# Moving the split activations hh and hl to lower SBUF addresses in a four-layer float32 stack

## The reference, cut to what matters

```python
def first_block(x, ...):
    for l in range(DEPTH):                       # DEPTH = 2
        h = rms_norm(x, mix_pre_norm[l])
        m = hybrid_mixer(h, w_in[l], ...)        # h @ w_in, three branches, gates, @ w_out
        x = x + rms_norm(m, mix_post_norm[l])
        h = rms_norm(x, ffn_pre_norm[l])
        x = x + rms_norm(swiglu(h, ffn_gate[l], ffn_up[l], ffn_down[l]), ffn_post_norm[l])
    return x

def second_block(x, positions, ...):
    for l in range(DEPTH):
        u = rmsnorm(h, attn_norm[l])
        h = h + hybrid_mixer_2(u, pos, w_in[l], ...)
        u = rmsnorm(h, mlp_norm[l])
        h = h + jnp.square(jax.nn.relu(u @ w_up[l])) @ w_down[l]
    return rmsnorm(h, final_norm)
```

## Time and profile before

| what | value |
|---|---|
| median of 3 executions | 2028.76 us |
| lowest and highest of them | 2018.31 and 2033.37 us |
| the profiled execution's own time | 2028.76 us |
| span of its instructions | 2026.9 us |
| PE busy | 1940.7 us (96%) |
| PEld busy | 1864.6 us (92%) |
| DVE busy | 1256.0 us (62%) |
| ACT busy | 994.6 us (49%) |
| POOL busy | 342.3 us (17%) |
| mean granted TensorE clock | 0.984 |
| read from HBM | 305.12 MB |

### The profile page before, as it was taken

One profiled execution on the slowest core, in us unless ns is written; L12 is line 12 of the kernel. 1 busy time (PEld: TensorE's weight loads), 2 busy tenths in 40 slices (PEclk: granted clock), 3 DMA queues, 4 the chain that ended last, 5 costly groups with the idle time before them and its releaser, 6 DMA issues.

```text
span 2026.9 us, 36388 instructions
## 1 busy us (share of the span) xinstructions
PE 1940.7 (96%) x15552; PEld 1864.6 (92%) x15552; DVE 1256.0 (62%) x1609; ACT 994.6 (49%) x1431; POOL 342.3 (17%) x186
## 2 busy tenths in 40 slices
PE   7999998999899999989998999999999999989998
PEld 7989998999888989989997889899999889989997
DVE  6864665665577455666637684476646685566643
ACT  5633455544464434654544444646535444555532
POOL 1150321000114112210002342220001242220000
PEclk9999999999999999999999999999999999999999
DMA  5422343656343333545653433345555433335552
GB/s 216 162 103 96 132 149 127 207 192 207 112 144 130 105 104 126 198 153 177 201 170 125 157 134 116 125 156 186 189 187 177 153 130 125 125 130 192 186 188 97
DMA packets 84544, 308.53 MB, mean 152 GB/s; under 512 B 9376, under 2 KB 9760, under 8 KB 84000
## 3 DMA queue, kind: packets, MB, share of 16 engines
q1 hardware_dynamic: 84384, 306.21, 44.5%
HBM read 305.12 MB, written 1.05 MB: 151 GB/s over the span
## 4 chain that ended last, share of the span: by engine, by line
PE 74%; DVE 15%; ACT 5%; issue 3%; POOL 1%; DMA 0%; SPq 0%; ACTq 0%; DVEq 0%; POOLq 0%
PE bank L1851 73%; DVE wlo L1034 6%; DVE area L1034 5%; DVE area L1040 2%; ACT whi L581 2%; ACT area L575 2%; DVE xT L1034 1%; POOL area L1628 1%; PE bank L2275 1%; PE bank L1989 1%; DVE FL L1034 0%; ACT L575 0%; DVE hl L1040 0%; ACT hh L575 0%; DVE B0L L1034 0%
## 5 line engine op out<-in xcount | busy, mean ns | idle before, releaser
L1034 DVE TENSOR_TENSOR wlo<-raw,whi 128x1024 fp32r<-128x1024 f32 x512 | 661.1, 1305 | 455.2 <-ACT whi L581 454.6
L1851 PE MATMUL bank<-hh,whi 128*128 128x256 f32 x2928 | 848.4, 290 | 43.6 <-DVE hl L1040 24.0
L1851 PE MATMUL bank<-hl,whi 128*128 128x256 f32 x2928 | 825.1, 282 | 0.0
L1851 PE MATMUL bank<-hh,wlo 128*128 128x256 f32 x2928 | 824.8, 282 | 0.0
L581 ACT CAST whi<-raw 128x1024 fp32r<-128x1024 f32 x572 | 588.2, 1046 | 352.0 <-PE bank L1851 346.8
L1851 PEld LDWEIGHTS bank<-hh,whi 128*128 128x128 f32 x2928 | 562.8, 192 | 61.2 <-issue 36.3
L1851 PEld LDWEIGHTS bank<-hl,whi 128*128 128x128 f32 x2928 | 560.1, 191 | 6.4 <-issue 6.2
L1851 PEld LDWEIGHTS bank<-hh,wlo 128*128 128x128 f32 x2928 | 559.8, 191 | 0.0
L1628 POOL TENSOR_TENSOR area<-area 128x512 f32<-128x512 f32 (+7 forms) x92 | 146.6, 1602 | 1037.7 <-ACT area L575 695.5
L1851 PE MATMUL bank<-FH,whi 128*128 128x256 f32 x1120 | 314.9, 281 | 5.3 <-DVE FL L1034 5.3
L1851 PE MATMUL bank<-FL,whi 128*128 128x256 f32 x1120 | 312.6, 279 | 0.0
(11 more groups left out here) (117 smaller groups left out, 1681.4 us busy)
## 6 DMA issues: line engine op xcount, KB each, us to landing
raw<-in_weights SPq DMA_DIRECT2D x572, 512.0 KB, 3.8
cst<-in_const SPq DMA_DIRECT2D x1, 1252.0 KB, 10.1
cst<-in_const SPq DMA_DIRECT2D x1, 1088.5 KB, 5.7
xT<-in_x SPq DMA_DIRECT2D x4, 256.0 KB, 5.6
out<-xT SPq DMA_DIRECT2D x1, 1024.0 KB, 3.8
area<-in_lev SPq DMA_DIRECT2D x2, 384.0 KB, 7.3
small<-in_small SPq DMA_DIRECT2D x2, 288.0 KB, 5.2
par<-in_par SPq DMA_DIRECT2D x1, 138.0 KB, 4.1
```

Of the source, the lines that this page charges most:

```text
L1034: return v.tensor_tensor(dst, x, y, op)
L1851: return e.matmul(ps, x, y, start=start, stop=stop, skip_group_check=skip)
```

## The change

The change moves the lines of `hh`, `hl` and `RSB` in the list of `sb` calls. No other line differs.

```diff
         xT = sb("xT", [P, 8, T])
+        hh = sb("hh", [P, 8, T], F32R)
+        hl = sb("hl", [P, 8, T], F32R)
         raw = sb("raw", [P, RAW, 1024])
         whi = sb("whi", [P, RING, 1024], F32R)
         wlo = sb("wlo", [P, RING, 1024], F32R)
         cst = sb("cst", [P, N_CONST])
         par = sb("par", [P, N_PAR])
         small = sb("small", [P, N_SMALL])
+        RSB = sb("RSB", [P, T])
         RST = sb("RST", [P, 2])
-        hh = sb("hh", [P, 8, T], F32R)
-        hl = sb("hl", [P, 8, T], F32R)
-        RSB = sb("RSB", [P, T])
         SW = sb("SW", [P, 8, 16], F32R)
```

## The result

The changed kernel takes 2047.59 us (median of 4, 2046.48 to 2048.51) against 2026.7 us of the kernel before (median of 4, 2018.31 to 2033.37): a ratio of 1.0102, 95% interval 1.0083 to 1.0122. It is slower by 1%, where no change was forecast. Its profiled execution took 2045.73 us, with a span of 2043.9 us against 2026.9.

The account below looks back on a forecast made before the run. The prediction took PE, with 74% of the chain of waits, nearly all in the weight matmuls, as the bound. Every term was 0, so with a small pull towards the earlier mean of 2026.8 it forecast 2027 us, range 2005 to 2048.

Parts of the forecast that it names:

- I take 0 for the address and leave the pace to the restarts: Matmuls on hh and hl: their new SBUF start costs 0; restarts after waits choose the pace, bounds -32.4 to +20.5 us.
- The address term of the matmuls: Matmuls streaming hh and hl: effect of their start moving from remainder 192 to 0, taken as 0.
- The view: Windows where PE never idles: two paces, 113.2 and 117.5 ns per matmul, on one layout, one kept until the next wait.
- rival A: Matmul and weight-load streams: equal remainders or new distances let them interlock at the fast pace; 2005 us, chance 0.15.
- The swapped rows: Matmuls streaming weights while hh is loaded: 115 ns per 256 columns, giving the address +1.8 to -2.5 ns, taken as 0.
- Rival B: Matmuls on hh and hl: each pays 4.35 ns for meeting the weight load; +28 us, 2055 us; 0.15 including rival C's tail.
- rival C: PE restarts: every one locks at the slow pace; at most +20.5 us, 2047 us; mostly inside the forecast's 0.70.
- The terms at 0 outside PE: ACT and DVE writes of hh and hl, DVE reads of RSB, the subtraction into wlo: moved addresses cost 0.
- The prediction's reading of the restarts: PE after each wait: matmuls and weight loads take up one of two stable interlocks, 4.35 ns per matmul apart, until the next.

Follow-up runs that it names:

- hi0: Against the kernel before: hh and hl stay in the upper half, but at remainder 0 by 256 like the weights; 2049.3 us, ratio 1.0164.
- both192: Against the changed kernel: cst, par, small and RST placed ahead of hh, so hh, hl, raw, whi, wlo start at remainder 192; 2067.07 us, ratio 1.0259.
- rsb: Against the kernel before: only RSB moved, from remainder 192 to 160, ahead of RST and hh; 2016.27 us, ratio 1.0018.
- d224: cst, par, RST and 32 free bytes between wlo and hh, putting hh, hl and FH at difference 224; 2051.75 us, ratio 1.018 to the kernel before.
- flip: Against the changed kernel: hh and hl unmoved, raw, whi and wlo moved to remainder 192; 2055.78 us, ratio 1.0197 to the kernel before.
- hl0: hl placed behind wlo at difference 0 from the weights, hh still at remainder 192; one execution, 2034.86 us against the kernel before's 2012.93.
- hh0: hh placed behind wlo at difference 0 from the weights, hl still at remainder 192; one execution, 2032.24 us against the kernel before's 2012.93.

## Why the prediction was wrong

The step that failed is "I take 0 for the address and leave the pace to the restarts". The address term of the matmuls is not 0. The mean record on `hh` and `hl` rose by 4 ns, 8784 x 4 ns = 35 us, while `FH`, through a luckier draw of paces in that execution, gave back 3360 x 2 ns = 7 us. PE busy rose by 1966.8 - 1940.7 = 26.1 us, and 17.0 us of them reached the end of the span. The other 9.1 us came off PE's idle time, which fell from 86.2 to 77.1 us: 5.3 of them are its wait for `wlo`, from 19.5 to 14.2, and DVE's share of the chain fell by 6 points.

The size is in part the luck of the first set. Against a fast draw of the kernel before, the step is 120.0 - 113.3 = 6.7 ns and not 4, and the same difference cost 1.64% in hi0's set, whose kernel before had a median of 2014.06 us.

What misled it, point by point.

- The view was right and its conclusion too wide. Two paces on one layout do show that the layout alone doesn't choose between them. They don't show that the layout has no part in which paces there are. With difference 192 there are two, 113 and 118; with difference 0 the windows show one, 120 (changed kernel, hi0, both192). My argument against rival A was used against the address as such.
- The swapped rows were no bound. They bracket 0 for another form, with 512 columns streamed past one load, and I wrote myself that no row showed the form with equal remainders. That other form did not become slower when it came to difference 0 itself. An unknown with 8784 instances behind it should have had its chance by the size of one seen step, 38 us, and not by the nearest row's sign.
- Rival B named the right mechanism in the right place, with the right control: a third pace, above 117.5, on `hh` and `hl` alone, `FH` untouched. Its price was 28 us from 4.35 ns and a share of 74%; the measured values are 4 ns and 17.0 / 26.1 = 65% of PE's added time. Its ground was half right: the distance of 32768 bytes is nothing (hi0 has 35584 and the same loss), the equal remainder by 256 is all. It had 0.15 together with the tail of C, much too little.
- The rule of the Trainium skill that was set against B ("TensorE: Matmul & The Clock Gate", "Step-by-step: what each phase is for": two read ports, so that a weight load takes nothing from the running matmul) does not hold here as far as it was used against B. Where the weights start relative to the streamed tile moves the pace from 113 to 120 ns, and it does so in stretches in which nothing but PE and its weight loads works. The measurement decides.
- The terms at 0 outside PE were right: `hh` 500 ns, `hl` 484 to 485, RSB no effect (rsb: 1.0018, 0.9996 to 1.004).
- The measured 2047.59 us lies just within the range, whose upper end of 2048 was set for rival C, at 2047 (its +20.5 us is already past the 20.3 us that the prediction calls 1%). That is luck. C has `hh` and `FH` alike at the slow pace; the windows have `hh` at 120 ns, which C doesn't know, and 443 matmuls on `FH` in 1490:1540, the fast pace. The kernel before is the odd one there with 427: in every other trace with `FH` at 192 the same window holds 441 to 444.
- The prediction's reading of the restarts, on which C rests, fits what was seen. Kernels with the two paces on `hh` scatter most (before 2018.31 to 2033.37, rsb 2013.24 to 2031.97); those without scatter less (after 2046.48 to 2048.51, d224 2050.56 to 2054.43, flip 2052.34 to 2057.09, both192 2065.31 to 2071.26), though from only four executions each, where rsb has ten. That a restart makes the choice is read from the timeline; no run set it.

That the stream meets PE's own weight load, and no other user of these tensors, is shown by the stretches without DMA packets and without work of DVE, ACT and POOL, in which the pace is 120 ns all the same. What happens between the two reads is not shown: the traces give the pace and nothing of the inside of PE or SBUF.

Still open: why 192 alone has the fast pace in the windows, and whether a start within a step of 32 bytes, or separate remainders for `whi` and `wlo` (they had one in every run), would keep the fast pace at every restart.

## What to carry to other kernels

Where every float32r matmul of 256 columns has its own weight load, as here, the SBUF starts of the streamed and the stationary tensors belong to the tuned state: note their difference by 256, and after any edit that shifts an allocation compare the distance between matmul starts before reading anything else into a change of 1 to 2%. Here one step of 32 bytes, from 192 to 224, cost 1.8%. Before a small change is called a gain or a loss, the kernel before needs many executions: this one's own reach over 1%. And a price that no row shows, multiplied by thousands of instances, belongs in the forecast's chances and not in its zeros.

## What the runs showed of the hardware that I had not expected

- The pace of 256-column float32r matmuls, each with its own 128 x 128 weight load, at a granted clock of 1.00, depends on the difference of the two SBUF starts by 256. From start to start in the windows: 113.3 or 117.8 ns at 192, 120.0 at 0 and 96, 116.7 at 32, 117.8 at 64, 118.7 or 120.0 at 128, 117.3 at 160, 118.3 at 224. The pace of 120.0 stays when no DMA packet moves and DVE, ACT and POOL are idle (1702.30:1703.20 of the changed kernel).
- At difference 192 the same stream runs at one of two paces, held over a thousand matmuls, 4.35 ns apart by the windows; the profiled executions of before and rsb lie 14.5 us apart, and PE's busy time by as much.
- hl0 and hh0, one execution each: with one of two streamed tensors at a bad difference, no window on `hh` and `hl` shows the fast pace.
